# A Conformer convolution branch: one of VectorE's five tap tiles goes to GpSimd, the norm's root is taken by token, channels go in pairs, output chunks in another order

## What is computed

```python
def conformer_conv(h, w_in, b_in, w_dw, b_dw, ln_g, ln_b, w_out, b_out):
    a, g = jnp.split(h @ w_in + b_in, 2, axis=-1)
    u = a * jax.nn.sigmoid(g)
    u = lax.conv_general_dilated(u, w_dw[:, None, :], window_strides=(1,),
        padding=[(CONV_WIDTH - 1, 0)], feature_group_count=D_MODEL) + b_dw
    ...
    mu = jnp.mean(u32, axis=-1, keepdims=True)
    var = jnp.mean(jnp.square(u32 - mu), axis=-1, keepdims=True)
    u = (u32 - mu) * lax.rsqrt(var + LN_EPS) * ln_g + ln_b
    return jax.nn.silu(u) @ w_out + b_out
```

## Time and profile before

| | |
|---|---|
| median of 3 runs (lowest to highest) | 3807.11 us (3806.42 to 3813.32) |
| the profiled execution's own time | 3808.92 us |
| its span | 3807.1 us |
| busy: PE, DVE, ACT, POOL | 83%, 63%, 42%, 20% of the span |
| chain that ended last: PE, DVE, DMA, ACT | 54%, 18%, 17%, 7% of the span |

### The profile page before, as it was taken

One profiled execution on the slowest core, in us unless ns is written; L12 is line 12 of the kernel. 1 busy time (PEld: TensorE's weight loads), 2 busy tenths in 40 slices (PEclk: granted clock), 3 DMA queues, 4 the chain that ended last, 5 costly groups with the idle time before them and its releaser, 6 DMA issues.

```text
span 3807.1 us, 43089 instructions
## 1 busy us (share of the span) xinstructions
PE 3164.7 (83%) x14762; PEld 1927.8 (51%) x14762; DVE 2393.8 (63%) x5191; ACT 1602.3 (42%) x4583; POOL 745.1 (20%) x797
## 2 busy tenths in 40 slices
PE   5898977788896876777787877777799989999899
PEld 2495533233351231222255433233497879898798
DVE  3444678555567777544456888776665866565564
ACT  1432455565555555655541111112233543334433
POOL 0000233233323333333201333333100000000000
PEclk8998999899997888888889999999999989999999
DMA  7665999899999999999926999999754235454354
GB/s 305 267 251 211 354 406 404 347 396 409 410 378 396 387 390 381 422 404 421 390 86 271 397 403 418 411 411 421 281 184 167 81 131 194 169 198 170 135 177 155
DMA packets 164409, 1160.02 MB, mean 305 GB/s; under 512 B 18817, under 2 KB 19585, under 8 KB 27522
## 3 DMA queue, kind: packets, MB, share of 16 engines
q0 software_dynamic: 110592, 805.36, 51.9%
q1 hardware_dynamic: 53634, 352.40, 25.0%
HBM read 1155.58 MB, written 2.10 MB: 304 GB/s over the span
## 4 chain that ended last, share of the span: by engine, by line
PE 54%; DVE 18%; DMA 17%; ACT 7%; issue 4%; POOL 0%; SPq 0%; DVEq 0%; ACTq 0%; POOLq 0%
PE ps L1320 9%; PE ps L1322 9%; PE ps L1321 9%; PE ps L1258 6%; PE ps L1230 4%; DMA rows<-in_peer,diag 4%; DMA h_ctx<-in_peer,idx 4%; PE ps L1179 3%; DMA rows<-in_peer,idx 3%; PE ps L1125 3%; DVE rows L2374 2%; PE ps L923 2%; DMA wring<-in_peer,diag 2%; DMA kvmem<-in_peer,diag 2%; PE ps L1151 1%
## 5 line engine op out<-in xcount | busy, mean ns | idle before, releaser
L2374 DVE CUSTOM_DVE_ANT_0 rows<-rows,ps 128x1024 f32<-128x1024 f32 x303 | 364.1, 1219 | 273.6 <-DMA rows<-in_peer,diag 186.9
L1320 PE MATMUL ps<-hT_hi,w_hi 128*128 128x256 f32 x1792 | 508.5, 284 | 8.9 <-DVE hT_lo L2496 8.9
L1322 PE MATMUL ps<-hT_lo,w_hi 128*128 128x256 f32 x1792 | 507.6, 283 | 0.0
L1258 PE MATMUL ps<-rows,diag 128*32 128x512 f32 x1212 | 370.2, 703 | 163.3 <-ACT diag L1842 157.9
L1321 PE MATMUL ps<-hT_hi,w_lo 128*128 128x256 f32 x1792 | 505.5, 282 | 0.0
L2865 POOL DMA_INDIRECT rows<-in_peer,diag x303 | 287.6, 949 | 980.8 <-PE ps L1258 598.8
L1320 PEld LDWEIGHTS ps<-hT_hi,w_hi 128*128 128x128 f32 x1792 | 342.5, 191 | 14.4 <-issue 14.3
L2486 DVE TENSOR_TENSOR w_lo<-wring,w_hi 128x2048 fp32r<-128x2048 f32 x120 | 274.7, 2291 | 112.6 <-ACT w_hi L1901 110.9
L1321 PEld LDWEIGHTS ps<-hT_hi,w_lo 128*128 128x128 f32 x1792 | 342.2, 191 | 0.1
L1322 PEld LDWEIGHTS ps<-hT_lo,w_hi 128*128 128x128 f32 x1792 | 341.1, 190 | 0.0
L1230 PE MATMUL ps<-rows,diag 128*128 128x512 f32 x512 | 246.6, 632 | 75.8 <-ACT diag L1826 68.7
(11 more groups left out here) (368 smaller groups left out, 6325.6 us busy)
## 6 DMA issues: line engine op xcount, KB each, us to landing
wring<-in_wgu SPq DMA_DIRECT2D x66, 1024.0 KB, 4.8
wring<-in_wdn SPq DMA_DIRECT2D x33, 1024.0 KB, 4.8
wring<-in_wG SPq DMA_DIRECT2D x32, 1024.0 KB
wring<-in_wmod SPq DMA_DIRECT2D x28, 1024.0 KB
wring<-in_wpq SPq DMA_DIRECT2D x24, 1024.0 KB
rows<-in_wgu SPq DMA_DIRECT2D x22, 1024.0 KB, 4.8
rows<-in_wmod SPq DMA_DIRECT2D x20, 1024.0 KB, 7.6
rows<-in_wdn SPq DMA_DIRECT2D x11, 1024.0 KB, 4.8
```

The source lines that it names most:

```text
L1258: ins = pe.matmul(ps[qd:qd + QUAD, UPB + half, :], quad_w[:, n % GROUP, :], spread_place(n)[:, D + half * 512:D + (half + 1) * 512], start ...
L1320: pe.matmul(out_, lh[l_at], rh[r_at], start=start, stop=False, skip_group_check=skip)
L1322: return pe.matmul(out_, lh[l_at], rl[r_at], start=False, stop=stop, skip_group_check=skip)
L2374: dve.tensor_tensor_reduce(out=down, in0=down, in1=h_ps, scale=1.0, scalar=0.0, op0=ALU.mult, op1=ALU.add, accum_out=a8[:, c:c + 1]).then_ ...
```

## The change

GpSimd takes tile 2: a multiplication into one of three scratch slices for each tap, and an addition of that slice to the sum, 61 instructions, which wait on one another through `pool_step`. VectorE keeps tiles 0, 1, 3 and 4. TensorE's sum for the mean takes tile 2 fifth. The variance is now summed per token onto the token's own partition (squares as the stationary operand, one column of the matrix of ones as the moving one), GpSimd takes the power -1/2 of 128 x 2 numbers, VectorE spreads them on two diagonal matrices, and TensorE multiplies these by the matrix of ones, so that the root stands on every partition again, in PSUM. Subtraction, squares, scaling and splitting go by two tiles in place of four. The chunks of `cout` go 0, 2, 1, 3, and the products wait for each pair of tiles.

```diff
+TAPS_POOL = 2
+OUT_ORDER = (0, 2, 1, 3)
...
-            plan += [("cwout", (c,)) for c in range(4)]
+            plan += [("cwout", (c,)) for c in OUT_ORDER]
...
+                    for k in range(4):
+                        if ready is not None and half == 0 and ts[0] == 0:
+                            ready(4 * c + k)
...
+                    for n in chunks:
                         ws[n] = chunk2()
+                        part(n, range(TT) if n == chunks[0] else (0,))
+                    for n in chunks[1:]:
+                        part(n, (1,))
...
+                for n, c in enumerate((0, 1, 3, 4, TAPS_POOL, 5, 6, 7)):
+                    if c == TAPS_POOL:
+                        pe.wait_ge(pool_y, 1)
+                    elif c < TAPS_DVE:
+                        pe.wait_ge(conv_y, n + 1)
...
-                    pe.wait_ge(ln_v, c // 4 + 1)
-                    last = pe.matmul(b[:, 0:TOK], ones, usq[:, c, :], start=(c == 0), stop=(c == 7))
+                    pe.wait_ge(ln_v, c // 2 + 1)
+                    for t in range(TT):
+                        last = pe.matmul(bs[t][:, 0:1], usq[:, c, t * P:(t + 1) * P], ones[:, 0:1], start=(c == 0), stop=(c == 7))
...
+            def inverse():
+                b = job2(("inv",))
+                for t in range(TT):
+                    pe.wait_ge(ln_g, t + 1)
+                    last = pe.matmul(b[:, t * P:(t + 1) * P], ones, inv_diag[:, t, :], start=True, stop=True)
+                ended(last, ("inv",))
...
+                run = by_tile("cv", conv_2, bout_b, lambda k: pe.wait_ge(ln_s, k // 2 + 1), OUT_ORDER)
+                inverse()
                 run()
...
-                todo = [(c, j) for j in range(TAPS) for c in (0, 1)] + [(c, j) for j in range(TAPS) for c in range(2, TAPS_DVE)]
+                todo = [(c, j) for j in range(TAPS) for c in (0, 1)] + [(c, j) for j in range(TAPS) for c in (3, 4)]
...
+                scaled(0)
+                gained(0)
+                for g in range(4):
+                    if g < 3:
+                        scaled(g + 1)
...
+                    parts(g)
+                    if g < 3:
+                        gained(g + 1)
...
+                pool.wait_ge(conv_u, c + 1)
+                own(pool.tensor_scalar(uc[:, c, :], upad[:, c, 0:TOK], vec2[:, 16 + c:17 + c], vec2[:, 264 + c:265 + c], ALU.mult, ALU.add))
+                own(pool.tensor_scalar(usq[:, 1, :], upad[:, c, 1:1 + TOK], vec2[:, 24 + c:25 + c], None, ALU.mult))
+                for j in range(2, TAPS):
+                    w = 16 + j * 8 + c
+                    if j > 3:
+                        pool.wait_ge(pool_step, step[0] - 2)
+                    own(pool.tensor_scalar(usq[:, j % 3, :], upad[:, c, j:j + TOK], vec2[:, w:w + 1], None, ALU.mult))
+                    pool.wait_ge(pool_step, step[0] - 1)
+                    own(pool.tensor_tensor(uc[:, c, :], uc[:, c, :], usq[:, (j - 1) % 3, :], ALU.add))
...
+            def conv_root():
+                pool.wait_ge(ln_q, TT)
+                pool.tensor_tensor(ln_inv, ln_var, minus_half[:, 0:TT], ALU.pow).then_inc(ln_r, 1)
```

More of the change, by code:

```diff
@@ L654, in build @@
         bout_b, vec2 = m0[:, 0:D], m0[:, D:D + 288]
[L655 to L656 removed]
+        ln_var, ln_inv = rl2[:, 0:TT], rl2[:, TT:2 * TT]
+        inv_diag = rln.rearrange("p (t n) -> p t n", t=TT)
         ones = rows[:, 3, 0:P]
@@ L1406, in dn, with by_tile @@
                     part(c, 1)
-            def by_tile(tag, lhs, bias=None, ready=None):
+            def by_tile(tag, lhs, bias=None, ready=None, chunks=range(4)):
                 keys = {(t, half): ("d", tag, t, half) for t in range(TT) for half in range(2)}
@@ L1415, in by_tile, with part @@
                         pe.matmul(b, sel[0:1, 0, :], bias[0:1, half * 512:(half + 1) * 512], start=True, stop=False, skip_group_check=True)
-                def part(n, t):
+                def part(n, ts):
                     half, c = divmod(n, 2)
+                    last = {}
                     for k in range(4):
[L1420 to L1427, removed]
+                        if ready is not None and half == 0 and ts[0] == 0:
+                            ready(4 * c + k)
+                        for t in ts:
+                            last[t] = product(bs[t, half], lhs, np.s_[:, 4 * c + k, t * P:(t + 1) * P], ws[n], np.s_[:, k * 512:(k + 1) * 512],
+                                              start=(bias is None and c + k == 0), stop=(c == 1 and k == 3), skip=bias is not None)
+                    for t in ts:
+                        if c == 1:
+                            ended(last[t], keys[t, half])
+                        elif t == TT - 1:
+                            ended(last[t], ("d", tag, "part", half))
+                        if t == TT - 1:
+                            chunk2_end()
                 def run():
-                    for n in range(4):
+                    for n in chunks:
                         ws[n] = chunk2()
[L1432 to L1437, removed]
+                        part(n, range(TT) if n == chunks[0] else (0,))
+                    for n in chunks[1:]:
+                        part(n, (1,))
                 return run
@@ L2606, in ln @@
             def ln():
-                halves = [slice(4 * half, 4 * half + 4) for half in range(2)]
+                two = [slice(2 * g, 2 * g + 2) for g in range(4)]
                 b = at_mm(dve, ("mean",))
-                bc = b[:, 0:TOK].unsqueeze(1).broadcast_to([P, 4, TOK])
-                for cs in halves:
+                bc = b[:, 0:TOK].unsqueeze(1).broadcast_to([P, 2, TOK])
+                for cs in two:
                     dve.tensor_tensor(uc[:, cs, :], uc[:, cs, :], bc, ALU.subtract).then_inc(ln_d, 1)
-                dve.wait_ge(ln_d, 2)
+                dve.wait_ge(ln_d, 4)
@@ L2613, in ln @@
                 dve.sem_inc(bank_free[job_bank["mean",]], 1)
[L2614 to L2628, removed]
+                for t in range(TT):
+                    b = at_mm(dve, ("var", t))
+                    dve.tensor_scalar(ln_var[:, t:t + 1], b[:, 0:1], LN_EPS, None, ALU.add).then_inc(ln_q, 1)
@@ new lines, in ln, with scaled @@
+                dve.wait_ge(ln_q, TT)
+                for t in range(TT):
+                    dve.sem_inc(bank_free[job_bank["var", t]], 1)
+                dve.wait_ge(ln_r, 1)
+                for t in range(TT):
+                    dve.tensor_scalar(inv_diag[:, t, :], ident[:, :], ln_inv[:, t:t + 1], float(D), ALU.mult, ALU.mult).then_inc(ln_g, 1)
+                y = at_mm(dve, ("inv",))[:, 0:TOK].unsqueeze(1).broadcast_to([P, 2, TOK])
+                dve.wait_ge(ln_v, 4)
+                def scaled(g):
+                    dve.tensor_tensor(uc[:, two[g], :], uc[:, two[g], :], y, ALU.mult).then_inc(ln_d, 1)
@@ L2629, in ln, with gained, parts @@
+                def gained(g):
+                    dve.wait_ge(ln_d, 5 + g)
+                    for c in (2 * g, 2 * g + 1):
                         dve.tensor_scalar(usq[:, c, :], uc[:, c, :], vec2[:, 272 + c:273 + c], vec2[:, 280 + c:281 + c], ALU.mult, ALU.add).then_inc(ln_z, 1)
-                    dve.wait_ge(ln_z, 4 * half + 4)
-                    dve.wait_ge(ln_t, 4 * half + 4)
+                def parts(g):
+                    cs = two[g]
+                    dve.wait_ge(ln_z, 2 * g + 2)
+                    dve.wait_ge(ln_t, 2 * g + 2)
```

34 lines of the change are left out of this document (23 added, 11 removed).

## The result

The changed kernel takes 3818.9 us (median of 20 runs, 3810.45 to 3825.68), the kernel before in the same runs 3810.62 us (median of 20). The ratio is 1.0019, 95% interval 1.0012 to 1.0025: slower by about 7.2 us (the medians lie 8.3 apart). The profiled execution took 3815.88 us, its span 3814.1.

What follows compares the result with a forecast made beforehand. VectorE's taps were taken to bound the kernel, late by 8 us. +18.5 us before the mean and -3.6 behind it gave +14.9 on 3808.92, so 3823.8, put at 3822 us for the median; range 3794 to 3837.

Steps and rivals of the forecast that it cites:

- What bounds the kernel: Before the mean: VectorE's taps bound, late by 8 us; anything taken beyond that leaves TensorE's taps as the bound.
- first rival: Taps: GpSimd reads beside VectorE without holding it up; mean 8.8 us earlier, 3794.7 us in all; chance 0.22.
- What GpSimd's work costs: Taps: GpSimd's 61 instructions add their whole length, 0.548 us each, 33.4 us, to VectorE's time; taps end 18.5 us later.
- The second rival: Taps: GpSimd holds the port for part of its instruction, 0.18 to 0.43 us; -7.6 to +7.6 us; chance 0.20.
- The mean in its old 4.1 us: After VectorE's taps: the mean follows in 4.1 us as before, TensorE again coming from an idle time.
- The variance: From mean to variance's end: 7.9 us before, now -0.9 us (-2.5 to +1.2), with 32 one-column records.
- The root: After the variance: spreading waits behind TensorE's 3.7 us bias, 4.3 us in all; -1.1, or +2.6 at the low clock.
- fourth rival: Behind the mean: TensorE stays at the low clock through one-column matmuls and bias; +2.2 for -3.6, 3827.8 us; no separate chance.
- Root to first product: From the root to the first product of `cout`: two tiles in place of four take 3.9 us for 6.8, -2.9 us.
- The products: Products of `cout`: TensorE waits 1.4 us for the third chunk's split, ready at 11.2 us; put at +1.3 us.
- The sum behind the mean: Variance, root, way to the first product and products together: -3.6 us, bounds -5.2 and +2.2.
- The signs named beforehand: Trace signs: taps near 0.9 us apart, last near 3049, TensorE waiting some 20 us, first product 8 us after the variance.

Runs made afterwards that it cites:

- e5: The changed kernel with the running sums of VectorE's four tiles kept in PSUM until the last tap, GpSimd's taps unchanged: 3799.72 us, ratio 0.9968 to the kernel before.
- e4: The changed kernel with GpSimd's 61 tap instructions replaced by fills that write SBUF and read nothing, tile 2's taps left out: 3799.82 us, one run.
- e3: The changed kernel with the four bias matmuls of the output product moved ahead of the mean: 3810.91 us, ratio 1.0001 to the kernel before.
- e8: The changed kernel with the output chunks in their old order 0, 1, 2, 3: 3815.36 us, one run.
- e7: The changed kernel with tile 2's taps back on VectorE and the bias moved ahead of the mean: 3802.4 us, ratio 0.9984 to the kernel before.
- e9: As e5, with all four bias matmuls between the mean and the variance: 3801.94 us, ratio 0.9966 to the kernel before.
- e1: The kernel before with only GpSimd's taps of tile 2 and the new order of the mean: 3814.7 us, ratio 1.0012 to the kernel before.
- e6: The changed kernel with tile 2 back on VectorE and its five tiles summed in PSUM, no GpSimd taps: 3807.53 us, one run.

## Why the prediction was right, and where not

The sign was right and the time near (3822 forecast, 3818.9 measured), but that is in part luck. Two errors of opposite sign lie under it: the forecast was +14.9 us, by the table it is +6.75. And the kernel before came out 3.5 us slower in these runs than in the three that I had built on (3810.62, 3807.11).

- **What bounds the kernel: right.** VectorE is late by 8 us, and what is taken from it beyond that only makes TensorE's taps the bound: in e5 they bound, and the mean ends 8.82 us earlier, the 8.8 of the first rival. VectorE's saving of 12.3 us is 12.2 to 12.3 in e4 and e5.
- **What GpSimd's work costs: the kind right, the size wrong.** The two exclude each other where both read SBUF. The step that failed is "exclude each other for their whole length": I took the whole instruction as its price, 0.548 us. The second rival, by which only a part of GpSimd's instruction keeps VectorE out, fits what was measured. GpSimd's instructions are longer than that (0.73 and 0.93 us unhindered in e5), but each takes only 0.33 from VectorE (0.22 for a multiplication, which reads one tensor, 0.48 for an addition, which reads two). 61 x 0.33 = 20.1, less 2.6 for the pauses, less 12.3, is +5.2; measured +5.45, forecast +18.5. The Trainium skill's rule in "SBUF — State Buffer", section "Who interferes with whom", names the pair rightly, and two exceptions that e4 and e5 bear out: a GpSimd instruction that only writes, and a VectorE instruction with at most one SBUF input. It makes the second with a proviso, "outside the 2-port perf modes"; whether the first taps, which were held up, run in such a mode, no run shows. The exclusive lock that it states agrees with what VectorE's split does to GpSimd (2.65 us for an addition); the other way VectorE lost 0.22 and 0.48 us to instructions of 1.09 and 0.84.
- **"If VectorE's unbroken taps never let GpSimd in":** it did not come to that; they let it in from tap to tap.
- **TensorE's and ScalarE's taps 6 us later: wrong.** TensorE's end at 78.83 in every kernel; TensorE is busy 67.20 of 67.20 us in GpSimd's stretch. Nothing hung on it.
- **The mean in its old 4.1 us: 1.04 short.** It took 5.15; its last six tiles ran at 0.50 throughout, behind 12.42 us of idling instead of 6.58.
- **The variance:** -1.46 us, forecast -0.9.
- **The root: wrong by 4.0 us.** Forecast -1.1, measured +2.89. The step put the bias at 3.70 us; it ran at the low level and took 7.12, the case that the step itself priced at +2.6 (fourth rival). e3 shows that this, and not VectorE's and GpSimd's trip, sets the time: 2.70 us without the bias.
- **Root to first product:** -2.80, forecast -2.9.
- **The products: the number right, its way not.** +1.32, forecast +1.3 as a wait for the split of the third chunk, ready 10.99 us behind the first product (forecast 11.2). The change has no such wait: 12 products run at the low level where 6 did before, and six times some 0.2 us make up nearly all of the 1.3. The split only sets how much a better clock could have given. That the other order of the chunks hides VectorE's last two pairs fell with e8: in the old order none is waited for.
- **The sum behind the mean:** -1.46 + 2.89 - 2.80 + 1.32, and 0.31 in the transposes, is +0.27 where -3.6 was forecast. What happened is the second rival's price (0.18 to 0.43 us) with the bias of the fourth rival on top: by the formula 61 x 0.33 - 18.5 = +1.6, plus 4.0 for the root and 1.04 for the mean, 6.7. So with TensorE's clock as forecast in the bias and the mean, this price would have left next to no change: e3, with the bias out of the way, ends the branch 0.74 us behind the kernel before. I gave the second 0.20 and had the row that spoke for it: 74 ns lost to a read of one element.
- **The signs named beforehand** are mostly against it. "Less than 0.43 us or more than 0.8" was to show it wrong, and GpSimd's instructions last 1.09 and 0.84. Tap to tap is 0.63 us on average (1.88 / 3) and not 0.9, the last tap ends at 3033.25 and not 3049, TensorE waits 12.42 us and not some 20, and the first product comes 12.30 us behind the variance, as before (12.20), and not 8. The spreading of the root does stand right behind the bias.

Left open: what sets TensorE's level in the bias. It ran high behind the taps in e7 and behind the mean in e9, but 5.04 us, 0.72 on average, behind the taps in e3, and 4.57 us in e1, where it stands as before (3.70).

## What to carry to other kernels

Work given to GpSimd beside VectorE is priced by what it takes from VectorE, not by its own length; moving one of VectorE's two SBUF inputs to PSUM can make it free, here 17 us in the branch between the change and e5. A step that is put elsewhere in TensorE's order can run at another clock there: price it at both levels, and look for an idle time elsewhere on that engine before putting it on the way. A gain shows only as far as the next thing late, so ask of each stage what would be waited for if the engine were faster: the third chunk's split took back every gain of clock in the products.

## What the runs showed of the hardware

- GpSimd's multiplication of 128 x 256 by a number per partition (0.93 us unhindered, 1.09 beside the taps) is longer than its addition of two tensors (0.73 and 0.84). The Trainium skill's figure for an addition of 2048 elements, in "GPSIMD Engine Reference", section "Performance versus the Vector engine", scaled to 256, had given an estimate of 0.56.
- VectorE's tap accumulates in PSUM at the pace of SBUF: 0.392 us from tap to tap in e5 and e6, 0.397 before.
- A VectorE tap of two SBUF inputs loses 0.22 us to GpSimd's multiplication and 0.48 to its addition, and nothing to a fill (e4: 0.396 us from tap to tap beside fills); with one of the inputs in PSUM it loses nothing (e5).
- Eight bias records of one partition by 512 columns take 3.70 us at a granted clock of 1.00 and 7.12 to 7.19 at 0.50; behind the eight at 1.00 the one-column records of e9 run at 0.63.
